# An MoE decoder trunk on one core: expert matrices in halves, zeros ahead of the last expert, and a scatter that closes the sums

## The reference

```python
g_star = argmax(x @ wg + bg)                     # one of 4 groups
top_val, top_idx = top_k(e_logits of that group, 2)   # 2 of its 8 experts
def expert_block(args):
    xb, e = args
    return (jax.nn.silu(xb @ w1[e]) * (xb @ w3[e])) @ w2[e]
# w1[e], w3[e]: 1024 x 512, w2[e]: 512 x 1024; y is weighted by the gate and summed per token
```

## Time and profile before

| | |
|---|---|
| median of 3 executions | 1427.2 us (1423.23 to 1430.21) |
| the profiled execution | 1425.7 us |
| its span, first to last instruction | 1423.7 us |
| mean granted TensorE clock | 0.921 |
| PE busy | 1155.6 us (81%) |
| DMA moved | 477.38 MB, mean 335 GB/s |
| chain that ended last, by engine | PE 52%, DMA 41% |

### The profile page before, as it was taken

The page is one execution under the profiler, slowest core; times in us unless marked ns, Lnnn a source line. Parts: engine busy times, 40 slices in busy tenths (PEclk is TensorE's granted clock), DMA queues, the critical chain, the costliest instruction groups (busy, mean ns, idle before and its releaser), DMA issues.

```text
span 1423.7 us, 33070 instructions
## 1 busy us (share of the span) xinstructions
PE 1155.6 (81%) x11866; PEld 726.1 (51%) x11867; DVE 397.5 (28%) x1046; ACT 169.1 (12%) x473; POOL 38.5 (3%) x81
## 2 busy tenths in 40 slices
PE   8999999988696686758789999989986665767665
PEld 7884458555453343334448858655543333334332
DVE  1963532342222121112133133252221111111113
ACT  1202502101010010001020001111110000000001
POOL 4000000001000000000000000000000000000000
PEclk9999999999899898889899999999999888888887
DMA  9746107679999999999995646454999999999994
GB/s 311 270 178 237 60 30 293 252 299 412 429 429 428 429 428 428 429 428 429 428 407 215 237 177 266 177 208 194 419 428 427 429 429 428 429 428 428 428 429 202
DMA packets 64823, 477.38 MB, mean 335 GB/s; under 512 B 4189, under 2 KB 11677, under 8 KB 39949
## 3 DMA queue, kind: packets, MB, share of 16 engines
q1 hardware_dynamic: 62572, 469.97, 80.5%
q0 software_dynamic: 2208, 6.81, 1.5%
HBM read 473.62 MB, written 3.15 MB: 335 GB/s over the span
## 4 chain that ended last, share of the span: by engine, by line
PE 52%; DMA 41%; issue 3%; DVE 2%; ACT 1%; SPq 0%; ACTq 0%; POOL 0%; DVEq 0%
DMA ring<-in_moe_w_dram 41%; PE bank L550 13%; PE bank L985 11%; PE bank L571 8%; PE bank L1001 3%; PE bank L752 2%; PE bank L1009 2%; PE bank L558 2%; PE bank L971 2%; PE bank L520 1%; PE bank L873 1%; PE bank L891 1%; PE bank L992 1%; PE bank L939 1%; PE bank L928 1%
## 5 line engine op out<-in xcount | busy, mean ns | idle before, releaser
L985 PE MATMUL bank<-ring,xT 128*32 128x256 f32 x4672 | 352.8, 468 | 205.2 <-DMA ring<-in_moe_w_dram 202.9
L985 PEld LDWEIGHTS bank<-ring,xT 128*32 128x32 f32 x4672 | 192.6, 133 | 359.7 <-issue 238.1
L550 PE MATMUL bank<-xT,ring 128*128 128x256 f32 x720 | 157.1, 379 | 0.7 <-PE bank L550 0.7
L550 PEld LDWEIGHTS bank<-xT,ring 128*128 128x128 f32 x720 | 136.3, 190 | 19.4 <-issue 1.1
L1001 PE MATMUL bank<-slot,xT 128*32 128x256 f32 x2336 | 140.4, 381 | 2.7 <-DVE xT L1543 2.4
L1533 DVE SCALAR_TENSOR_TENSOR xT<-xT,bank 64x256 f32<-64x256 f32 x73 | 30.3, 415 | 371.9 <-ACT xT L1776 371.9
L571 PE MATMUL bank<-ring,slot 128*128 128x512 f32 x256 | 111.5, 593 | 4.0 <-ACT slot L1750 2.0
L1009 PE MATMUL bank<-xT 32*128 32x256 f32 x1200 | 87.4, 405 | 24.1 <-issue 22.9
L1001 PEld LDWEIGHTS bank<-slot,xT 128*32 128x32 f32 x2336 | 77.5, 110 | 54.4 <-issue 9.4
L1519 DVE TENSOR_TENSOR xT<-iota,place 128x64 f32 (+1 forms) x73 | 16.5, 226 | 275.0 <-issue 272.5
L1776 ACT ACTIVATE xT<-bank 64x256 f32<-64x256 f32 x73 | 27.5, 377 | 541.8 <-PE bank L985 524.0
(11 more groups left out here) (275 smaller groups left out, 826.5 us busy)
## 6 DMA issues: line engine op xcount, KB each, us to landing
ring<-in_moe_w_dram SPq DMA_DIRECT2D x126, 2048.0 KB, 33.5
slot<-in_moe_w_dram SPq DMA_DIRECT2D x64, 2048.0 KB, 38.2
ring<-in_od_w_in_dram SPq DMA_DIRECT2D x6, 2048.0 KB, 20.8
ring<-in_xa_wq_dram SPq DMA_DIRECT2D x4, 2048.0 KB, 11.3
ring<-in_xa_wo_dram SPq DMA_DIRECT2D x4, 2048.0 KB, 11.4
ring<-in_ev_w_in_dram SPq DMA_DIRECT2D x3, 2048.0 KB, 14.6
ring<-in_mem_wk_dram SPq DMA_DIRECT2D x2, 2048.0 KB, 15.1
ring<-in_mem_wv_dram SPq DMA_DIRECT2D x2, 2048.0 KB, 10.7
```

The source lines that it names most:

```text
L550: ins = mm(ps, w[:, k, c0:c0 + P], rhs[:, k, :], start=(k == 4), stop=(k == 3))
L985: ins = mm(b1[qs[2 * m + h], 0:S], xg[:, k, :], ws[m][:, k, h, :, :], start=(k == 0), stop=(k == KC - 1))
```

## The change

`load_expert` replaces the single DMA. w1 still comes in one. w3 and w2 come in two DMAs of half the columns: the first 2048 floats of each partition raise a new semaphore `first_half_in[s]`, the second 2048 raise `loaded[s]`. In w3 the first half holds chunks k = 0 to 3 of 8, in w2 chunks c = 0 and 1 of 4. Hidden starts after w1 and w3's first half and waits for the whole of w3 ahead of k = 4. Results start after w2's first half and wait for the whole ahead of c = 2. In the last turn of the loop, ahead of hidden of expert 31, PE issues 8 matmuls of zeros into bank 6. The last scatter of a layer sets `stop=True` on its products of the second token tile and signals the banks itself; the four closing matmuls are gone.

```diff
+        first_half_in = [sem(f"first_half_in{i}") for i in range(SLOTS)]
...
+            def load_expert(s, m_, L, e):
+                src, half_ = expert_weights(PARTS[m_], L, e), 2048
+                if m_ == 0:
+                    sp.dma_start(slot_ap(s), src).then_inc(loaded[s], 16)
+                else:
+                    sp.dma_start(slot_ap(s)[:, 0:half_], src[:, 0:half_]).then_inc(first_half_in[s], 16)
+                    sp.dma_start(slot_ap(s)[:, half_:2 * half_], src[:, half_:2 * half_]).then_inc(loaded[s], 16)
...
-                        sp.dma_start(slot_ap(s), expert_weights(PARTS[m_], L, e + SETS)).then_inc(loaded[s], 16)
+                        load_expert(s, m_, L, e + SETS)
...
-                def hidden(fam, slots_, xg):
+                def hidden(fam, slots_, xg, whole):
...
                     for k in range(KC):
+                        if k == KC // 2:
+                            pe.wait_ge(loaded[slots_[1]], whole)
...
-                def results(fam, slot_):
+                def results(fam, slot_, whole):
...
                     for c in range(4):
+                        if c == 2:
+                            pe.wait_ge(loaded[slot_], whole)
...
-                def scatter(fam, cb, yy):
+                def scatter(fam, cb, yy, final=False):
...
-                                     start=False, stop=False, skip_group_check=True)
-                    ins.then_inc(fam.scattered, 1)
+                                     start=False, stop=final and t == TT - 1, skip_group_check=True)
+                            if final and t == TT - 1:
+                                filled(ins, ("f", 3 * L + 2, q))
+                    if not final:
+                        ins.then_inc(fam.scattered, 1)
...
-                    pe.wait_ge(loaded[s[1]], ready[1])
-                    hidden(fam, s, xgT)
+                    pe.wait_ge(first_half_in[s[1]], ready[3])
+                    hidden(fam, s, xgT, ready[1])
...
-                    pe.wait_ge(loaded[s[2]], ready[2])
+                    pe.wait_ge(first_half_in[s[2]], ready[4])
...
-                    results(fam, s[2])
+                    results(fam, s[2], ready[2])
...
                         at = ((j + 1) % SETS, i + (j + 1) // SETS)
+                        if j == (NE - 2) % SETS:
+                            with pe.If(i > TURNS - 2):
+                                keep_warm(banks[6], 8)
+                            pe.nop()
                         unit_hidden(moe_slots[L][at[0]], ready_at(*at), first + m + 1)
...
-                scatter(fam, comb, y)
-                for q in range(Q):
-                    filled(mm(acc[q][:, 0:8], zero16[:, 0:P], zero16[:, 0:8], start=False, stop=True, skip_group_check=True),
-                           ("f", 3 * L + 2, q))
+                scatter(fam, comb, y, True)
```

More of the change, by code:

```diff
@@ L294, in program @@
         bank_of, fills, rotation = {}, [0] * 8, [0]
-        moe_base, moe_slots = [], []
+        moe_base, half_base, moe_slots = [], [], []
+        half_uses = [0] * SLOTS
         def slot_ap(s):
@@ L433, in _ @@
                 moe_base.append(list(slot_uses))
+                half_base.append(list(half_uses))
                 slot_last[6] = (weights_used, order.index(f"wo_mix{L}b") + 1)
@@ L440, in _ @@
                         wait_free(s)
-                        sp.dma_start(slot_ap(s), expert_weights(PARTS[m_], L, j)).then_inc(loaded[s], 16)
+                        load_expert(s, m_, L, j)
                     if j == 1:
@@ L470, in _ @@
                         slot_uses[s] += e // SETS + 1
+                        half_uses[s] += e // SETS + 1 if m_ else 0
                         slot_last[s] = (used_up[m_], L, e)
@@ L1036, in unit_rest @@
                     gather(fam, disp)
-                    pe.wait_ge(loaded[s[2]], ready[2])
+                    pe.wait_ge(first_half_in[s[2]], ready[4])
                     pe.wait_ge(fam.comb_ready, n)
                     pe.wait_ge(fam.hidT_ready, n)
-                    results(fam, s[2])
+                    results(fam, s[2], ready[2])
                 def ready_at(j, i):
-                    return [(i + (moe_base[L][s] + 1)) * 16 for s in moe_slots[L][j]]
+                    whole = [(i + (moe_base[L][s] + 1)) * 16 for s in moe_slots[L][j]]
+                    return whole + [(i + (half_base[L][s] + 1)) * 16 for s in moe_slots[L][j][1:]]
                 unit_hidden(moe_slots[L][0], ready_at(0, 0), 1)
```

## The result

The changed kernel takes 1429.2 us (median of 20 runs) against 1426.4 for the kernel before, a ratio of 1.0021 [1.0014, 1.0029]: 3 us slower. (Ratios leave out runs disturbed from outside; two medians are not always those of the same runs.) Its profiled execution took 1428.8 us, span 1426.9.

A forecast was written before the change was run, and what follows sets the result against it. The prediction took 777 of 1423.7 us to be paced by how fast the 16 DMA engines move bytes. Its terms, 9.3 - 4.0 - 4.1 + 0.7 = +1.9 us on 1427.2, gave 1429.1 us, range 1419 to 1438.

The forecast's parts named there:

- part 1: Expert loops of both layers: split w3 and w2 make smaller packets at a fixed time each, +9.3 us.
- part 2: End of each layer: expert 31 starts on first halves, statistics come earlier, -4.0 us in layer 1, -4.1 in layer 0.
- The additional issues are no term: SP in the expert loops: two issues need 0.80 us, with 33 us of queue in front, so no cost.
- the case that I had priced at -3.0: Layer 0's end: hidden of expert 31 takes 5.35 us again instead of running at full speed, -3.0 us.
- The zeros: Ahead of expert 31's hidden: 1.8 us of matmuls, then idle 2 to 3.8 us in layer 1, under 1 in layer 0.
- Part 3: PE's loop ahead of the DMA-paced stretches: additional waits, branch and nop cost two turns a layer, +0.7 us.
- (a): Rival for the expert loops: packets of 8 KB cost nothing, -7.4 us, 1419.8 us; chance 0.16.
- (b): Rival: each of 106 more transfer ends stops the DMA engines; 5.3 us at 0.05 each, 1439.7 at 0.1; chance 0.12.
- (c): Rival for layer ends: zeros or cold clock undo hidden's earlier start, only 1 us a layer saved, 1435.2 us; chance 0.10.

The follow-up runs named there:

- halves alone: Kernel before with w3 and w2 in two column transfers, PE waiting for both before hidden and results, no zeros, old closing matmuls: 1434.5 us, 1.0065.
- the quarters: Kernel before with w3 and w2 in four column transfers (rows of 4 KB), PE waiting for all four, no zeros, old closing: 1450.4 us, 1.0163.
- one transfer and two rows: Kernel before with w3 and w2 each as 128 x 2 rows of 8128 bytes in one transfer with one completion, sums incomplete: 1435.6 us, 1.0060.
- the version that beats both: Against the changed kernel: halves for expert 31 alone, closing scatter kept, no zeros; 1420.8 us, 0.9959 of the kernel before.

## Why the prediction was right

It said 1429.1 us, +1.9 against before. Measured were 1429.2 us and +3.0 (ratio 1.0021 x 1426.4). That the time itself came out within 0.1 us is luck: the kernel before took 0.8 us less in the comparison than the 1427.2 that I had built on. That the difference came out within 1.1 us is luck in part: part 1 was 0.8 us too high and part 2 took 1.7 us too much off, and these errors partly cancel. What was right beside luck are the two mechanisms and their order of size.

- **Part 1, packets, +9.3.** Right. The halves alone cost 8.5 to 9.3 us; the price of a packet or completion is 8.5 to 8.9 ns instead of 9.8, and the line between 2 KB and 16 KB rows holds at 8 and at 4 KB within 15%. The rule of the Trainium skill (DMA: Bandwidth & Descriptors, Rules for kernel authors) that 1 MiB on 128 partitions gives the most bandwidth would have made it nothing; the trace decides against it for this size of change: 424 and 428 GB/s are both "full", and the difference is 8.5 us.
- **"The additional issues are no term."** The effect was right, the reason not. SP does not issue in 0.4 us each any more, it blocks 6.8 us for one. That cost nothing here: the DMA share stayed at 1.01, and at 1.02 with the quarters.
- **Part 2, the ends, -8.1.** The mechanism was right, the term too large: 3.5 + 2.9 = 6.4 us by the profiles, 6.3 by the two ratios. By the distance that I had named, w3's landing to the first statistics, it is 8.7 us in layer 0 and 8.8 in layer 1, where I had 7.5 and 8.4. Layer 0 makes most of the difference (-2.9 for -4.1): I took full clock there behind the zeros and the profile has 5.39 us, the case that I had priced at -3.0. The closing matmuls were counted at 0.5 us a layer, because the first quarter's sum is ready early; they are worth 0.13 (1.65 instead of 1.78 us) and show no effect alone.
- **The zeros.** I had the idle that is left in layer 1 at 2 to 3.8 us (2.96 measured) and hidden at 5.35 (5.16). For layer 0 I had under 1 us of idle behind them; it is 1.98, since PE was free 3.8 us ahead of hidden (729.4 to 733.19) where I had 2.7. The reading behind both was too simple: I took a pause ahead of hidden as what sets its clock, and the windows show the clock full in the pauses of 1.98 and of 2.67 us and falling inside hidden.
- **Part 3, +0.7.** Not shown: the loops of single profiles vary by 2 to 3 us. What the terms leave, 3.0 - 8.5 + 6.4 = 0.9, is of its size, but below what these runs can tell.
- **Rivals.** (a), packets of 8 KB for nothing, fell with the halves alone. (b), a price per transfer, fell with one transfer and two rows and with the earlier trace rows, which leave nothing for it. (c), ends that yield nothing, fell with the distance of 8.8 us.

## What to carry to other kernels

Where a stretch is paced by the DMA engines, as here, finer rows lengthen all of it (0.15 us for each expert), and their gain comes once, at its last transfers: cut only those (here -5.7 us instead of +3). Price finer rows beforehand by two rows of the trace with the queue full, one with long and one with short rows; the difference per packet is the term. And before adding work to hold the clock ahead of a last step, look at what the same change does to the step before it: in the version that beats both, the work of expert 30 itself is the filler.

## What the runs showed of the hardware

- With w3 and w2 in transfers to 64 partitions each, rows of 16 KB and a DMA share of 1.01, the loop moves 217 GB/s where transfers to 128 move 428; w1's transfers to 128 partitions stand in the same queue and are as slow. The Trainium skill (DMA: Bandwidth & Descriptors, Rules for kernel authors) advises against two transfers to disjoint partition halves since they serialize; serialized transfers at the full rate would have cost some 1 us here, and the runs show +53% (1.528). What halves the rate I did not test.
- Each packet costs 8.5 to 9 ns beside its bytes between rows of 4 KB and of 16 KB, if a completion write is counted as one packet (no run parts the two), 9.8 by the rows of 2 KB, and 14 with rows of 8128 bytes.
- In the loops SP blocks in the issue of a DMA: 6.78 us for one with rows of 8 KB, 8.18 us for two of 64 partitions with rows of 16 KB, and 0.4 in the kernel before. Neither the number of transfers nor that of packets explains both.
- In the same code ahead of the change the first 128 long matmuls take 27.64, 28.68 or 29.14 us from one profiled execution to another, and with the stretch from 142 to 157 us this makes 4.1 us at the first hidden, more than the 3.2 us by which the spans before and after differ.
- After eight matmuls of zeros and 2.96 us of idle, hidden ran at full clock in one kernel (3.66 us); after eight and 1.98 us in another the clock fell from 1.00 to 0.50 when hidden had run for 1.1 us (5.39). What decides is open.
